# Block 1's head norm: four of six tiles centred by one product and normalised inside the last pass of the pairs

## What is computed

```python
y = rwkv7_recurrence(rf, heads(decay), heads(k), vf, kk, heads(a))
mean = jnp.mean(y, axis=-1, keepdims=True)
var = jnp.mean(jnp.square(y - mean), axis=-1, keepdims=True)
yn = ((y - mean) * lax.rsqrt(var + GN_EPS)).reshape(B, S, RWKV_WIDTH)
yn = yn * lnx_w + lnx_b
return ((yn + bonus) * gate) @ w_a
```

## Time and profile before

| | us |
|---|---|
| median of 3 runs | 2122.12 |
| the profiled execution, its own time | 2121.97 |
| its span in the profile | 2119.9 |
| third pass, from L1971 to the copy of tile 5 | 412.1 to 455.4 |
| head norm and barrier, from there to the first product of stage 4 | 455.4 to 489.2 |

### The profile page before, as it was taken

The page is one execution under the profiler, slowest core; times in us unless marked ns, Lnnn a source line. Parts: engine busy times, 40 slices in busy tenths (PEclk is TensorE's granted clock), DMA queues, the critical chain, the costliest instruction groups (busy, mean ns, idle before and its releaser), DMA issues.

```text
span 2119.9 us, 36738 instructions
## 1 busy us (share of the span) xinstructions
PE 1969.2 (93%) x14820; PEld 1889.4 (89%) x14820; DVE 1409.8 (67%) x2225; ACT 909.6 (43%) x1358; POOL 100.6 (5%) x162
## 2 busy tenths in 40 slices
PE   7897889977799999999999999999999999899997
PEld 7896789966799999998888999998999878888997
DVE  6995576755766567746656677757774565667764
ACT  3433434413455444434445444434443444444442
POOL 0201031000000000003000000000000300000000
PEclk7998888977999999999999999999999999999999
DMA  8683110003355544543222444543554323254552
GB/s 343 259 316 106 40 41 1 1 21 122 109 189 193 184 140 167 192 157 130 80 103 90 149 148 171 192 165 139 178 182 156 130 80 112 92 175 150 187 196 102
DMA packets 43447, 301.40 MB, mean 142 GB/s; under 512 B 4736, under 2 KB 6928, under 8 KB 11072
## 3 DMA queue, kind: packets, MB, share of 16 engines
q1 hardware_dynamic: 42736, 296.90, 39.8%
q0 software_dynamic: 592, 2.87, 0.4%
HBM read 298.70 MB, written 1.05 MB: 141 GB/s over the span
## 4 chain that ended last, share of the span: by engine, by line
PE 76%; DVE 12%; DVEq 4%; ACT 3%; issue 3%; DMA 1%; POOL 0%; ACTq 0%; POOLq 0%; SPq 0%
PE acc L698 20%; PE acc L700 19%; PE acc L699 19%; DVE w_lo L669 3%; ACT w_hi L662 2%; PE acc L2581 2%; PE mb L721 1%; PE acc L1989 1%; PE mb L1989 1%; DVEq L1405 1%; DVEq L845 1%; PE mb L2553 1%; DMA land<-in_w_out 1%; DVE upd L794 1%; DVE gla_sq L2919 1%
## 5 line engine op out<-in xcount | busy, mean ns | idle before, releaser
L698 PE MATMUL acc<-h_hi,w_hi 128*128 128x272 f32 (+1 forms) x2960 | 873.9, 295 | 51.6 <-DVE w_lo L669 24.7
L700 PE MATMUL acc<-h_hi,w_lo 128*128 128x272 f32 (+1 forms) x2960 | 855.4, 289 | 0.0
L699 PE MATMUL acc<-h_lo,w_hi 128*128 128x272 f32 (+1 forms) x2960 | 854.1, 289 | 0.0
L662 ACT ACTIVATE w_hi<-land 128x2048 fp32r<-128x2048 f32 (+2 forms) x251 | 482.0, 1921 | 490.5 <-PE acc L700 424.1
L669 DVE TENSOR_TENSOR w_lo<-land,w_hi 128x2048 fp32r<-128x2048 f32 (+2 forms) x251 | 576.8, 2298 | 171.2 <-ACT w_hi L662 170.7
L698 PEld LDWEIGHTS acc<-h_hi,w_hi 128*128 128x128 f32 x2960 | 569.8, 193 | 66.4 <-DVE w_lo L669 27.6
L699 PEld LDWEIGHTS acc<-h_lo,w_hi 128*128 128x128 f32 x2960 | 569.5, 192 | 1.9 <-issue 0.2
L700 PEld LDWEIGHTS acc<-h_hi,w_lo 128*128 128x128 f32 x2960 | 569.7, 192 | 0.0
L698 PE MATMUL acc<-a_hi,w_hi 128*128 128x272 f32 (+1 forms) x880 | 251.8, 286 | 0.8 <-DVE w_lo L669 0.5
L699 PE MATMUL acc<-a_lo,w_hi 128*128 128x272 f32 (+1 forms) x880 | 250.3, 284 | 0.0
L700 PE MATMUL acc<-a_hi,w_lo 128*128 128x272 f32 (+1 forms) x880 | 250.3, 284 | 0.0
(11 more groups left out here) (519 smaller groups left out, 2508.6 us busy)
## 6 DMA issues: line engine op xcount, KB each, us to landing
land<-in_w_gu SPq DMA_DIRECT2D x110, 1024.0 KB, 4.8
land<-in_w_in SPq DMA_DIRECT2D x65, 1024.0 KB, 4.9
land<-in_w_down SPq DMA_DIRECT2D x40, 1408.0 KB, 6.0
ada_first<-in_w_ada SPq DMA_DIRECT2D x24, 1024.0 KB, 8.2
land<-in_w_ab SPq DMA_DIRECT2D x24, 512.0 KB, 3.5
land<-in_w_out SPq DMA_DIRECT2D x12, 1024.0 KB, 4.9
land<-in_w_in_single SPq DMA_DIRECT2D x6, 512.0 KB, 3.5
const<-in_const POOLq DMA_DIRECT2D x1, 1134.0 KB, 8.5
```

The costliest lines, as they stand in the source:

```text
L662: k.nc.scalar.activation(k.w_hi[:, p.par, 0:size * P], k.land[:, p.par, 0:size * P], ACT.Copy).then_inc(k.hi_ready, 1)
L698: mm(out, k.w_hi[:, par, c], hi, start=start, stop=False)
L699: mm(out, k.w_hi[:, par, c], lo, start=False, stop=False)
L700: return mm(out, k.w_lo[:, par, c], hi, start=False, stop=stop)
```

## The change

A centring matrix (identity less a 64th of the ones of each head) is made in `beta[:, 0]` once. In the third pass tiles 0 to 3 (`EARLY` = 4) are centred by one product of 512 columns for two tiles, after rounds 0 and 1; ACT squares them and scales them by `lnx_w` in rounds 1 and 2; PE sums the squares after round 3; ACT takes the root in round 4; DVE takes the reciprocal in round 4, between its two streams; PE spreads it behind the mfn products. `bon` gets `lnx_b` (ACT, after the rounds) and both it and `c1` get `gate` (DVE, ahead of the output copies), and DVE multiplies and adds for the four tiles between the copies of tile 4 and tile 5. Tiles 4 and 5 go through the same steps at the end. The order of the affine step changes: `c * gate * spread + (bon + lnx_b) * gate`.

```diff
+EARLY = RT - 2
+def pe_norm_early(k, pe, r):
+    mm = k.nc.tensor.matmul
+    if r < 2:
+        if r == 0:
+            pe.wait_ge(k.gn_in, 1)
+        mm((k.mb, k.acc)[r][:, 2, :], k.beta[:, 0, 0:P],
+           k.c1[:, 2 * r:2 * r + 2, :].rearrange("p t n -> p (t n)"), start=True, stop=True).then_inc(k.gn_sum, 1)
+    if r == 3:
+        pe.wait_ge(k.gn_sq, 2)
+        for t in range(EARLY):
+            last = mm(k.mb[0:32, 2, 0:SEQ], k.sel[:, t * 32:(t + 1) * 32], k.kap[:, t, :],
+                      start=t == 0, stop=t == EARLY - 1)
+        last.then_inc(k.gn_sum, 1)
+def pe_norm_spread(k, pe, n, tiles, banks):
+    pe.wait_ge(k.gn_inv, n)
+    for i, t in enumerate(tiles):
+        last = k.nc.tensor.matmul(banks[i // 2][:, (i % 2) * SEQ:(i % 2 + 1) * SEQ],
+                                  k.spread[:, t * P:(t + 1) * P], k.per_head[:, :], start=True, stop=True)
+    last.then_inc(k.gn_spread, 1)
 def pe_rwkv_pairs(k, pe):
...
+            if j == PAIRS - 1:
+                pe_norm_early(k, pe, r)
...
             pe.wait_ge(k.rt_copied, nth(j, 1, 0, s))
+            if j == PAIRS - 1:
+                pe.wait_ge(k.gn_root, 1)
...
             last.then_inc(k.mfn_mm, 1)
+        if j == PAIRS - 1:
+            pe_norm_spread(k, pe, 1, tuple(range(EARLY)), (k.mb[:, 1, :], k.acc[:, 1, :]))
 def act_rwkv_pairs(k, act):
...
     for j in range(PAIRS):
+        if j == PAIRS - 1:
+            a(k.warm[:, 0:1], k.eps[:, 1:2], ACT.Sqrt)
...
+                if j == PAIRS - 1:
+                    act_norm_early(k, act, r, s)
+        if j == PAIRS - 1:
+            for t in range(RT):
+                last = a(k.bon[:, t, :], k.bon[:, t, :], ACT.Identity, bias=vec(k, "lnx_b", t))
+            last.then_inc(k.gn_norm, 1)
 def dve_rwkv_pairs(k, dve):
...
+        if j == PAIRS - 1:
+            stt(k.beta[:, 0, 0:P], const(k, "pair_ones"), -1.0 / HD, const(k, "ident"), ALU.mult,
+                ALU.add).then_inc(k.gn_in, 1)
...
+                if j == PAIRS - 1 and r == ROUNDS - 2 and s == 1:
+                    dve.wait_ge(k.gn_root, 1)
+                    v.reciprocal(k.per_head[:, :], k.per_head[:, :]).then_inc(k.gn_inv, 1)
                 dve.wait_ge(k.round_mm, nth(j, ROUNDS, r, s))
...
+        if j == PAIRS - 1:
+            dve_norm_gated(k, dve)
         for s in STREAMS:
             output(j, s)
             if j < PAIRS - 1:
                 queries(s)
+            elif s == 0:
+                dve_norm_early(k, dve)
 def pe_rwkv_out(k, pe):
+    for t, bank in ((EARLY, k.mb), (EARLY + 1, k.acc)):
+        pe.wait_ge(k.y_evac, t + 3)
+        k.nc.tensor.matmul(bank[:, 2, 0:SEQ], k.beta[:, 0, 0:P], k.c1[:, t, :], start=True,
+                           stop=True).then_inc(k.gn_sum, 1)
+    for t in range(EARLY, RT):
+        pe.wait_ge(k.gn_sq, t - 1)
+        last = k.nc.tensor.matmul(k.mb[0:32, 0, 0:SEQ], k.sel[:, t * 32:(t + 1) * 32], k.kap[:, t, :],
+                                  start=t == EARLY, stop=t == RT - 1)
+    last.then_inc(k.gn_sum, 1)
+    pe_norm_spread(k, pe, 2, tuple(range(EARLY, RT)), (k.acc[:, 0, :],))
+def act_norm_early(k, act, r, s):
+    if r in (1, 2):
+        g, bank = r - 1, (k.mb, k.acc)[r - 1]
+        if s == 0:
+            act.wait_ge(k.gn_sum, g + 1)
+            k.nc.scalar.activation(k.kap[:, 2 * g:2 * g + 2, :],
+                                   bank[:, 2, :].rearrange("p (t n) -> p t n", t=2), ACT.Square)
+        else:
+            for t in range(2):
+                last = act_norm_scaled(k, 2 * g + t, bank[:, 2, t * SEQ:(t + 1) * SEQ])
+            last.then_inc(k.gn_sq, 1)
+    if r == 4 and s == 0:
+        act_norm_root(k, act, 3, k.mb[0:32, 2, 0:SEQ])
 def act_rwkv_out(k, act):
+    act.wait_ge(k.chain_evac, nth(PAIRS - 1, 3, 2, 1))
+    a(k.y1_hi[:, RT:KT, :], k.yb_keep[:, :, :], ACT.Copy)
+    act.wait_ge(k.gn_affine, 1)
+    a(k.y1_hi[:, 0:EARLY, :], k.c1[:, 0:EARLY, :], ACT.Copy).then_inc(k.gn_norm, 1)
+    for t, bank in ((EARLY, k.mb), (EARLY + 1, k.acc)):
+        act.wait_ge(k.gn_sum, t)
+        a(k.kap[:, t, :], bank[:, 2, 0:SEQ], ACT.Square).then_inc(k.gn_sq, 1)
+    act_norm_scaled(k, EARLY, k.mb[:, 2, 0:SEQ])
+    act_norm_scaled(k, EARLY + 1, k.acc[:, 2, 0:SEQ]).then_inc(k.gn_norm, 1)
+    act_norm_root(k, act, 6, k.mb[0:32, 0, 0:SEQ])
     prologue(split_hi, k, act, M_AB1, AB_K)
+    act.wait_ge(k.gn_affine, 2)
+    a(k.y1_hi[:, late, :], k.c1[:, late, :], ACT.Copy).then_inc(k.gn_norm, 1)
+def dve_norm_gated(k, dve):
+    dve.wait_ge(k.gn_sq, 2)
+    tt(k.c1[:, early, :], k.c1[:, early, :], k.gate[:, early, :], ALU.mult)
+    dve.wait_ge(k.gn_norm, 1)
+    tt(k.bon[:, :, :], k.bon[:, :, :], k.gate[:, :, :], ALU.mult)
+def dve_norm_apply(k, dve, n, tiles, banks):
+    dve.wait_ge(k.gn_spread, n)
+    for i, bank in enumerate(banks):
+        two = k.c1[:, tiles.start + 2 * i:tiles.start + 2 * i + 2, :]
+        tt(two, two, bank.rearrange("p (t n) -> p t n", t=2), ALU.mult)
+    dve.drain()
+    tt(k.c1[:, tiles, :], k.c1[:, tiles, :], k.bon[:, tiles, :], ALU.add).then_inc(k.gn_affine, 1)
 def dve_rwkv_out(k, dve):
+    dve.wait_ge(k.gn_norm, 2)
+    rest(early, k.c1[:, early, :])
+    dve.wait_ge(k.gn_norm, 3)
+    tt(k.c1[:, late, :], k.c1[:, late, :], k.gate[:, late, :], ALU.mult)
+    dve.wait_ge(k.gn_root, 2)
+    v.reciprocal(k.per_head[:, :], k.per_head[:, :]).then_inc(k.gn_inv, 1)
+    split_lo(k, dve, Panel.of(M_AB1), AB_K)
+    dve.drain()
+    dve_norm_apply(k, dve, 2, late, (k.acc[:, 0, :],))
+    rest(slice(RT, KT), k.yb_keep[:, :, :])
+    split_lo(k, dve, Panel.of(M_AB1 + 1), AB_K)
+    dve.wait_ge(k.gn_norm, 4)
+    rest(late, k.c1[:, late, :])
```

More of the change, by code:

```diff
@@ L2214, in dve_rwkv_pairs @@
                 queries(s)
+            elif s == 0:
+                dve_norm_early(k, dve)
 def pe_rwkv_out(k, pe):
-    pe_pair_sums(k, pe, k.gn_in, k.c1, k.gn_sum)
-    pe_head_sums(k, pe, k.gn_sq, k.tmp, 3, k.gn_sum)
-    pe_head_spread(k, pe, k.gn_inv, k.acc, k.gn_spread)
+    for t, bank in ((EARLY, k.mb), (EARLY + 1, k.acc)):
+        pe.wait_ge(k.y_evac, t + 3)
+        k.nc.tensor.matmul(bank[:, 2, 0:SEQ], k.beta[:, 0, 0:P], k.c1[:, t, :], start=True,
+                           stop=True).then_inc(k.gn_sum, 1)
@@ new lines, in pe_rwkv_out, with act_norm_root @@
+    for t in range(EARLY, RT):
[4 more added lines that the diff above has]
+    pe_norm_spread(k, pe, 2, tuple(range(EARLY, RT)), (k.acc[:, 0, :],))
+def act_norm_root(k, act, n, src):
+    act.wait_ge(k.gn_sum, n)
+    k.nc.scalar.activation(k.per_head[:, :], src, ACT.Sqrt, bias=k.eps[0:32, 1:2],
+                           scale=1.0 / HD).then_inc(k.gn_root, 1)
@@ new lines, in act_norm_scaled @@
+def act_norm_scaled(k, t, src):
+    return k.nc.scalar.activation(k.c1[:, t, :], src, ACT.Copy, scale=vec(k, "lnx_w", t))
+def act_norm_early(k, act, r, s):
[11 more added lines that the diff above has]
+        act_norm_root(k, act, 3, k.mb[0:32, 2, 0:SEQ])
@@ L2223, in act_rwkv_out @@
 def act_rwkv_out(k, act):
     a = k.nc.scalar.activation
-    act.wait_ge(k.y_evac, RT + 2)
-    prologue(split_hi, k, act, M_AB1, AB_K)
[L2227 to L2233, removed]
@@ L2234, in act_rwkv_out @@
-    act.wait_ge(k.gn_root, 2)
-    a(k.y1_hi[:, 0:RT, :], k.c1[:, :, :], ACT.Copy)
-    a(k.y1_hi[:, RT:KT, :], k.yb_keep[:, :, :], ACT.Copy).then_inc(k.gn_root, 1)
+    late = slice(EARLY, RT)
+    act.wait_ge(k.chain_evac, nth(PAIRS - 1, 3, 2, 1))
[5 more added lines that the diff above has]
+        a(k.kap[:, t, :], bank[:, 2, 0:SEQ], ACT.Square).then_inc(k.gn_sq, 1)
@@ new lines, in act_rwkv_out @@
+    act_norm_scaled(k, EARLY, k.mb[:, 2, 0:SEQ])
+    act_norm_scaled(k, EARLY + 1, k.acc[:, 2, 0:SEQ]).then_inc(k.gn_norm, 1)
+    act_norm_root(k, act, 6, k.mb[0:32, 0, 0:SEQ])
+    prologue(split_hi, k, act, M_AB1, AB_K)
+    act.wait_ge(k.gn_affine, 2)
+    a(k.y1_hi[:, late, :], k.c1[:, late, :], ACT.Copy).then_inc(k.gn_norm, 1)
+def dve_norm_gated(k, dve):
+    tt = k.nc.vector.tensor_tensor
+    early = slice(0, EARLY)
+    dve.wait_ge(k.gn_sq, 2)
+    tt(k.c1[:, early, :], k.c1[:, early, :], k.gate[:, early, :], ALU.mult)
+    dve.wait_ge(k.gn_norm, 1)
+    tt(k.bon[:, :, :], k.bon[:, :, :], k.gate[:, :, :], ALU.mult)
@@ new lines, in dve_norm_apply, with dve_norm_early @@
+def dve_norm_apply(k, dve, n, tiles, banks):
+    tt = k.nc.vector.tensor_tensor
+    dve.wait_ge(k.gn_spread, n)
[4 more added lines that the diff above has]
+    tt(k.c1[:, tiles, :], k.c1[:, tiles, :], k.bon[:, tiles, :], ALU.add).then_inc(k.gn_affine, 1)
+def dve_norm_early(k, dve):
+    dve.drain()
+    dve_norm_apply(k, dve, 1, slice(0, EARLY), (k.mb[:, 1, :], k.acc[:, 1, :]))
@@ L2241, in dve_rwkv_out, with rest @@
     tt = v.tensor_tensor
[L2242 to L2247, removed]
-    dve.drain()
[L2249 to L2262, removed]
+    early, late = slice(0, EARLY), slice(EARLY, RT)
+    def rest(tiles, src):
+        tt(k.y1_lo[:, tiles, :], src, k.y1_hi[:, tiles, :].bitcast(F32), ALU.subtract)
```

(5 more changed lines are left out.)

## The result

Runs of both kernels in turn: the changed kernel took 2099.33 us in the median of 6 (2094.8 to 2103.39), the kernel before 2121.84 (6 runs, 2111.13 to 2127.75); the ratio is 0.9899 [0.9871, 0.9926]. The profiled execution of the changed kernel took 2103.2, against 2121.97 for the profiled one of before: 18.8 less.

A forecast was written before the change was run, and what follows sets the result against it. A serial ladder of engines, 34.28 us from tile 5's copy to stage 4, was taken as the bound where the change lives. Tail -22.1 plus added work 4.7 gave -17.4, so 2121.97 became 2104.6 us; range 2100.5 to 2110.5.

The forecast's parts named there:

- Part 1: Work added inside the third pass, ahead of the output products: costs 4.7 us.
- (a): Two centring products of 512 columns on a full PE in the third pass's rounds: 1.7 us in all.
- (b): Four PE products for the sums of squares in the third pass, at full clock: 1.8 us in all.
- (c): DVE's reciprocal in round 4, waiting for ACT's root, makes the second stream's round 5 late: 1.0 us PE stall.
- (d): Spread of four tiles behind the mfn products, 1.75 us of PE work: makes the chain 0.3 us late.
- Part 2: Output products at half clock: DVE's moved gate and apply work fits its idle time before both copies; cost 0.
- Part 3: Tail from tile 5's copy to stage 4, at half clock: 12.2 us instead of 34.3, giving back 22.1.
- Part 4: Start of stage 4, 4.86 us at half before: expected the same; bounds a gain of 2.4, a loss of 1.
- rival A: Full clock lasts through the output products, so DVE binds there: 3.4 us less, 2101.2; chance 0.13.
- B: Round 5's new stall brings the clock down earlier, so some 6.5 us of work runs at half: 2110.1; chance 0.17.
- D: Clock falls in rounds 0 to 2 of the third pass and stays down: +25 us, 2130; chance 0.01.
- C: DVE's gate and apply work (5.7 us) isn't covered, or the tail's handoffs cost twice as much: 2109.5; chance 0.07.

The follow-up runs named there:

- uncovered: Changed kernel with DVE's gate and apply work of tiles 0 to 3 moved behind the copy of tile 5; median 2106.28 us, ratio to before 0.9932.
- after_again: The changed kernel, unchanged, run again for a second profile; median 2102.56 us in 6 runs, stretch 59.43 us.
- k128_fill: Changed kernel with the spread's operands zero-padded from 32 to 128 rows and two dummy products between chain and outputs; median 2096.06 us, on a second run 2097.27.

## Why the prediction was right and where it was wrong

**What bounds the kernel, right within the stretch.** The ladder was serial, and what left it was worth its length. That the rest of the kernel just moves up is not shown; see the Sum below.

**Part 1, right: 4.52 for 4.7.** From the first `akt` times `vt` product to the outputs it is 38.21 or 38.25 against 33.70. PE's own starts give the pieces: round 0 grew from 3.58 to 4.49, round 1 from 3.81 to 4.43, round 2 is 0.08 shorter, round 3 grew from 3.83 to 5.59, 3.2 in all for (a) and (b), forecast 3.4. T is 434.39, and the reciprocal starts at T + 1.29 and the second stream's round 5 at T + 3.46, where 1.3 and 3.5 were worked out; PE idles 0.86 for (c), forecast 1.0. The other 1.3 of the 4.52 are (c) and (d), 0.9 and 0.4, where 1.0 and 0.3 were forecast. What was costed at nothing was free: PE is busy 16.33 of 16.35 in rounds 0 to 3, so ACT's squares and copies held nobody up, and the root takes 0.47 with no table load ahead of it (the load, 1.28, stands at 397.10, in ACT's idle time). `bon`'s six instructions took 2.50 at 436.97 instead of at most 3.6, in ACT's idle time.

**Part 2, right in its cover, 0.5 too cheap.** DVE idles ahead of both copies; `uncovered` prices the cover at 5.7 to 6.6. Tile 5's copy starts at 459.97, forecast 459.7. But it comes 9.68 after the first output product, where it came 9.18 after it before. The prediction took 8.90 from a stretch that starts 0.7 us into the output products of before; their first 0.5 us still ran at full there, in three of the five profiles, and run at half now.

**Part 3, right in kind, 0.2 too cheap in the first profile and up to 0.7 too dear in the others.** The tail is 12.43 in the first profile (forecast 12.2, from 34.28) and 11.53 to 11.79 in the five others. The rung that differs is the spread. In the first profile it took 2.08, at half. PE's timeline and two stretches in `after_again`:

```profile
464.74 1.23 PE L1938 MATMUL acc<-per_head,spread 32*128 32x256 f32 x4 [2.33 <-DVE per_head L2361]
```
```profile
462.00:463.00 1.00, 0.41 (x2) 0.00 (x0) 0.55 (x2) 0.55 (x2) 0.00 (x0) 0.89 0.00 0
464.74:466.00 1.26, 1.23 (x4) 0.66 (x4) 1.02 (x1) 0.07 (x1) 0.00 (x0) 0.86 0.00 0
```

There the clock had come back at 462.2, with PE still busy (to 462.41) in the sums of squares. It stayed at full while PE waited for the root and the reciprocal, fell again in the spread's last 0.4 us, and the spread's four records took 1.23. In five of the six profiles the full level came back in the tail in this way for a while; only in the first it didn't. "At the half level" was the rarer case.

**Part 4, within its bounds.** Stage 4 ran 3.20 at half, where it had been 4.86: a gain of some 0.8. In `after_again` it was at half for some 5.5, a loss of some 0.3.

**The clock in the output part, right.** Half in all six profiles of the changed kernel. The Trainium skill (TensorE: Matmul & The Clock Gate, "HAM oscillation") puts the fall down to gaps in which PE is idle. The trace doesn't agree: the clock fell at the end of 445.88:448.40, in which PE was busy for all of 2.52, and PE's longest idle time ahead of it in the third pass was the 0.86 of round 5. In four of the five other profiles the clock fell 1.0 to 1.5 us later, where PE waits for DVE ahead of the output products. `k128_fill` shows the other side: rival A's mechanism is real and priced right in DVE's part, but takes an edit that this change doesn't have. B and D didn't happen: rounds and `wu` ran at 1.00. C is refuted by `uncovered`; its 2109.5 wasn't the sum of its own terms, since 2104.6 and 5.7 make 2110.3.

**What failed: the Sum, and the range made from it.** The step was "2121.97 - 17.4 = 2104.6. Its own range, by the bounds, is 2102.3 to 2107." It has two terms at nothing: what lies outside the stretch, which rests on "the rest of the kernel just moves up" alone, and the scatter of executions. What the runs showed in their place is 3.4 ± 1 us outside the stretch's 17.9, whose cause stays open, and a standard deviation of 3.4 to 3.8. From the forecast to the result:

| step | us |
|---|---|
| forecast | 2104.6 |
| the stretch gave 17.9, not 17.4 | -0.5 |
| the mean of before is 2122.2, not 2121.97 | +0.2 |
| outside the stretch, not located | -3.4 |
| mean of the changed kernel | 2100.9 |
| the six runs of the result, against that mean | -1.6 |
| result | 2099.3 |

The -1.6 is the luck of six executions: the mean of all 20 lies within the stated range, at its low end.

The bounds held the uncertainty of the edits alone. (Added all one way they make 2099.7 to 2109.8, and not 2102.3 to 2107; how the narrower range came about isn't said.) They had no term for how single executions scatter, 3.4 to 3.8 here, although the clock is granted differently each time and the three runs shown happened to lie within 2 us. A median of six moves by some 1.5 for that alone (3.4 over the root of 6 is 1.4). With such a term the low end would have been some 3 us lower, and the result inside. The forecast of the parts was good to 0.7 us; the forecast of the whole couldn't be.

## What to carry to other kernels

Where one engine after the other works and nothing overlaps, work that leaves the ladder is worth its full length; look for the cover in a part where another engine is slowed, and prove it by taking the cover away, as `uncovered` does. Price what is put into a full engine by its rows at the clock of that place, and a wait put into a queue by who stands behind it: both came out to within 0.3 us. But don't put the rest of the kernel at nothing only because its code is the same, add to every range the scatter between executions, from more than three of them, and don't read a difference of a few us out of single profiles.

## What was not expected of the hardware

- In the first profile half the clock came at the end of a stretch in which PE was never idle (2.52 of 2.52 busy, with 32-row products for 1.9 of it). With the same products at 128 rows and two more behind them, the full level was granted through the outputs in all three profiles: 5.05 for 9.61. With either edit alone it wasn't, in one profile each.
- The output products at half, 64 columns wide and busy 9.61 of 9.61, didn't bring the clock back. In the tail it came back at 462.2 of `after_again`, behind 256-column products that PE had run without a break since 458.6, and it then stayed at full while PE stood idle for 2.33.
- Executions of one program scatter by 3.4 to 3.8 us (standard deviation) of 2100, and go with the mean granted clock (correlation 0.85 and 0.87).
